# Tile 0's latent queries ahead of a half projection of tile 1 in layer 1, and five throw-away products left out

## The reference

```python
z = rms_norm(x) @ w_in            # 1184 columns: q, k, v of group A | latent queries cq (256) | ckv (128) | k_rope (32)
q_b = rms_norm(cq) @ b_w_uq       # 8 heads x 96, group B, multi-head latent attention
k_nope, v = split(ckv @ b_w_ukv)  # keys and values of group B out of the latent
o = concat(sliding_window_attention(q_a, k_a, v_a, sinks), latent_attention(q_b, k_nope, k_rope, v))
x = x + o @ w_o
x = x + swiglu(rms_norm(x))       # layer 0;  layer 1: top 2 of 8 SwiGLU experts, 2816 wide
```

## Time and profile before

| | |
|---|---|
| median of 3 runs | 1202.36 us (1201.98 to 1204.39) |
| profiled execution, own time | 1203.37 us |
| its span, first to last instruction | 1201.5 us |
| outside the span (difference) | 1.87 us |
| PE busy | 1179.6 us, 98% |
| DVE, ACT, POOL busy | 548.7, 329.9, 80.3 us |
| DMA | 348.56 MB, mean 290 GB/s |
| granted TensorE clock, mean | 0.999 |

### The profile page before, as it was taken

The page is one execution under the profiler, slowest core; times in us unless marked ns, Lnnn a source line. Parts: engine busy times, 40 slices in busy tenths (PEclk is TensorE's granted clock), DMA queues, the critical chain, the costliest instruction groups (busy, mean ns, idle before and its releaser), DMA issues.

```text
span 1201.5 us, 24345 instructions
## 1 busy us (share of the span) xinstructions
PE 1179.6 (98%) x10285; PEld 618.4 (51%) x10285; DVE 548.7 (46%) x1035; ACT 329.9 (27%) x612; POOL 80.3 (7%) x179
## 2 busy tenths in 40 slices
PE   8999999999999999999999999999999999999998
PEld 5566699999995566533333333333333333333254
DVE  2677534544414667533433434354264244334334
ACT  2576533443324556310210210210200200211101
POOL 4132000000001120000000000000000100100100
PEclk9999999999999999999999999999999999999999
DMA  9261294554530353999999999999999999999996
GB/s 304 60 168 37 92 285 150 174 175 132 162 125 1 63 132 125 352 369 375 406 389 413 398 399 413 399 398 414 399 396 415 399 399 415 390 408 414 392 410 256
DMA packets 114104, 348.56 MB, mean 290 GB/s; under 512 B 8592, under 2 KB 34032, under 8 KB 103808
## 3 DMA queue, kind: packets, MB, share of 16 engines
q1 hardware_dynamic: 108656, 335.55, 74.4%
q0 software_dynamic: 3648, 10.60, 3.1%
q10 hardware_dynamic: 1744, 1.61, 0.4%
HBM read 339.70 MB, written 8.04 MB: 289 GB/s over the span
## 4 chain that ended last, share of the span: by engine, by line
PE 86%; DMA 6%; DVE 4%; ACT 2%; SPq 1%; issue 1%; DVEq 0%; ACTq 0%
PE ps L2439 34%; PE ps L2446 17%; PE ps L2344 12%; PE ps L2075 8%; PE ps L2360 6%; DMA ring<-in_moe_w_gate 2%; DMA ring<-in_moe_w_down 2%; DMA ring<-in_w_in 2%; SPq L736 1%; PE ps L2274 1%; PE ps L2221 1%; PE ps L2236 1%; PE ps L2166 1%; PE ps L2155 1%; PE ps L2088 1%
## 5 line engine op out<-in xcount | busy, mean ns | idle before, releaser
L2439 PE MATMUL ps<-ring,xg 128*32 128x512 f32 (+1 forms) x1792 | 197.6, 547 | 1.2 <-DMA ring<-in_moe_w_gate 0.8
L1857 DVE STREAM_TRANSPOSE am<-act_m 32x256 f32<-32x256 f32 (+1 forms) x288 | 172.6, 599 | 4.7
L2439 PE MATMUL ps<-ring_more,xg 128*32 128x512 f32 (+1 forms) x1280 | 149.7, 571 | 0.0
L1351 DVE TENSOR_TENSOR w_lo<-ring,w_hi 128x2048 fp32r<-128x2048 f32 (+1 forms) x34 | 76.0, 2234 | 96.2 <-ACT w_hi L941 96.2
L2075 PE MATMUL ps<-ring,hT 128*128 128x512 f32 x256 | 115.4, 596 | 0.1
L2439 PEld LDWEIGHTS ps<-ring,xg 128*32 128x32 f32 x1792 | 58.0, 110 | 111.2 <-issue 106.4
L1842 DVE TENSOR_TENSOR act_m<-act_m,ps 64x512 f32<-64x512 f32 (+1 forms) x24 | 15.2, 635 | 213.1 <-ACT act_m L1290 213.1
L2439 PE MATMUL ps<-ring_more,am 128*32 128x512 f32 x896 | 108.9, 592 | 0.0
L2446 PE MATMUL ps<-ring,xg 128*32 128x512 f32 (+1 forms) x896 | 106.7, 547 | 0.0
L2344 PE MATMUL ps<-hT_hi,w_hi 128*128 128x288 f32 x352 | 104.3, 296 | 0.5 <-DVE hT_lo L1725 0.5
L2344 PE MATMUL ps<-hT_lo,w_hi 128*128 128x288 f32 x352 | 103.8, 295 | 0.0
(11 more groups left out here) (388 smaller groups left out, 1539.2 us busy)
## 6 DMA issues: line engine op xcount, KB each, us to landing
ring_more<-in_moe_w_down SPq DMA_DIRECT2D x64, 1024.0 KB, 16.0
ring<-in_moe_w_gate SPq DMA_DIRECT2D x48, 1024.0 KB, 17.0
ring_more<-in_moe_w_up SPq DMA_DIRECT2D x48, 1024.0 KB, 16.2
ring<-in_moe_w_gate SPq DMA_DIRECT2D x32, 768.0 KB, 18.6
ring_more<-in_moe_w_gate SPq DMA_DIRECT2D x16, 1024.0 KB, 14.7
ring<-in_moe_w_up SPq DMA_DIRECT2D x16, 1024.0 KB, 18.4
ring<-in_moe_w_down SPq DMA_DIRECT2D x16, 1024.0 KB, 15.5
ring<-in_moe_w_up SPq DMA_DIRECT2D x16, 768.0 KB, 14.7
```

The costliest lines, as they stand in the source:

```text
L1351: V.tensor_tensor(lo[:, 0:size], src[:, 0:size], hi[:, 0:size].bitcast(F32), ALU.subtract).then_inc(lo_ready, 1)
L1857: ins = V.transpose(am[GRAN * q:GRAN * q + GRAN, c % 2, 0:nk, GRAN * g:GRAN * g + GRAN], src)
L2439: ins = mm_(ps[GRAN * s_:GRAN * s_ + GRAN, b, 0:half], x[:, GRAN * g:GRAN * g + GRAN], w[:, half * h:half * h + half], start=(n == 0), sto ...
```

## The change

In layer 1 alone, three hand-written orders and one table are edited:

- PE: `(item, 4)` runs ahead of `(za, 1, 0, 1)`, and no longer behind it.
- ACT: `(isq, 4)` and `(ir, 4)` run ahead of `(zev, 1, 0)`, and `(ir, 4)` is no longer behind `(tie, 3)`.
- DVE: `(i2, 4)` runs ahead of `(sm, 1)`, and no longer behind it.
- `WAITING[1]` loses the entry for `(s, 2)`: five throw-away products, and the wait in front of them.

No step is added or dropped, and since `za` takes no small PSUM pair, every small step keeps its pair.

```diff
--- before.py
+++ after.py
@@ -113,8 +113,8 @@
              ("p", 7), ("o", 6), ("o", 7), ("hf", 0), ("wo", 1, 0, 0), ("wo", 1, 1, 1), ("wo", 1, 0, 1), ("hf", 1)],
             [("h", 0), ("tc",), ("item", 0), ("za", 0, 1, 0), ("h", 2), ("za", 2), ("titem", 0), ("za", 0, 0, 0), ("zc", 0),
              ("za", 0, 1, 1), ("za", 0, 0, 1), ("tq", 2), ("h", 1), ("item", 1), ("s", 0), ("za", 1, 0, 0), ("item", 2),
-             ("za", 1, 1, 0), ("tq", 0), ("za", 1, 1, 1), ("titem", 1), ("p", 0), ("item", 3), ("titem", 2), ("za", 1, 0, 1),
-             ("item", 4), ("titem", 3), ("s", 1), ("s", 2), ("titem", 4), ("o", 0), ("p", 1), ("s", 3), ("o", 1), ("zc", 1),
+             ("za", 1, 1, 0), ("tq", 0), ("za", 1, 1, 1), ("titem", 1), ("p", 0), ("item", 3), ("titem", 2), ("item", 4), ("za", 1, 0, 1),
+             ("titem", 3), ("s", 1), ("s", 2), ("titem", 4), ("o", 0), ("p", 1), ("s", 3), ("o", 1), ("zc", 1),
              ("ob", 1), ("p", 2), ("to", 2), ("o", 2), ("p", 3), ("wo", 2), ("o", 3), ("tq", 1), ("wo", 0, 0, 0), ("item", 5),
              ("item", 6), ("s", 4), ("wo", 0, 0, 1), ("titem", 5), ("s", 5), ("titem", 6), ("wo", 0, 1, 0), ("hf", 2), ("p", 4),
              ("s", 6), ("wo", 0, 1, 1), ("o", 4), ("p", 5), ("s", 7), ("ro", 2), ("o", 5), ("p", 6), ("wo", 1, 0, 0), ("o", 6),
@@ -131,8 +131,8 @@
               ("th", 2), ("th", 0), ("nh", 1), ("n2", 1), ("th", 1)],
              [("tce",), ("n1", 2), ("n1", 0), ("isq", 0), ("n1", 1), ("ir", 0), ("zev", 2), ("tie", 0), ("zr", 2), ("zcev", 0),
               ("zev", 0, 1), ("zev", 0, 0), ("tqe", 2), ("isq", 1), ("zr", 0), ("e", 0), ("ir", 1), ("isq", 2), ("tqe", 0),
-              ("ir", 2), ("zev", 1, 1), ("tie", 1), ("pe", 0), ("isq", 3), ("tie", 2), ("ir", 3), ("zev", 1, 0), ("isq", 4),
-              ("tie", 3), ("ir", 4), ("e", 1), ("tie", 4), ("pe", 1), ("e", 2), ("e", 3), ("zcev", 1), ("pe", 2), ("zr", 1),
+              ("ir", 2), ("zev", 1, 1), ("tie", 1), ("pe", 0), ("isq", 3), ("tie", 2), ("ir", 3), ("isq", 4), ("ir", 4), ("zev", 1, 0),
+              ("tie", 3), ("e", 1), ("tie", 4), ("pe", 1), ("e", 2), ("e", 3), ("zcev", 1), ("pe", 2), ("zr", 1),
               ("oe", 2), ("toe", 2), ("pe", 3), ("oe", 3), ("tqe", 1), ("n2", 2), ("isq", 5), ("ir", 5), ("isq", 6), ("ir", 6),
               ("tie", 5), ("e", 4), ("tie", 6), ("e", 5), ("pe", 4), ("e", 6), ("oe", 4), ("pe", 5), ("xd", 2),
               ("oe", 5), ("e", 7), ("pe", 6), ("oe", 6), ("pe", 7), ("n2", 0), ("oe", 7), ("xd", 0), ("xh", 2),
@@ -147,14 +147,14 @@
               ("hfd", 1), ("tl", 1)],
              [("hd", 0), ("x1", 2), ("hd", 2), ("i1", 0), ("i2", 0), ("r1", 0), ("r1", 1), ("set",), ("z1", 2), ("z2", 2),
               ("hd", 1), ("z1", 0), ("sm", 0), ("i1", 1), ("z2", 0), ("i2", 1), ("i1", 2), ("i2", 2), ("i1", 3), ("i2", 3),
-              ("i1", 4), ("sm", 1), ("i2", 4), ("sm", 2), ("od", 0), ("sm", 3), ("nm", 2), ("od", 1), ("z1", 1), ("nm", 3),
+              ("i1", 4), ("i2", 4), ("sm", 1), ("sm", 2), ("od", 0), ("sm", 3), ("nm", 2), ("od", 1), ("z1", 1), ("nm", 3),
               ("z2", 1), ("wd", 2), ("i1", 5), ("i2", 5), ("i1", 6), ("i2", 6), ("sm", 4), ("sm", 5), ("nm", 4), ("hfd", 2),
               ("nm", 5), ("sm", 6), ("wd", 0, 0), ("x2", 2), ("nm", 6), ("sm", 7), ("top", 2), ("wd", 0, 1), ("nm", 7),
               ("x2", 0), ("hfd", 0), ("wd", 1, 0), ("xl", 2), ("xl", 0), ("hfd", 1), ("top", 0), ("wd", 1, 1),
               ("hfdb", 1), ("rs", 1), ("x2h", 1), ("top", 1), ("x2", 1)]]
 
 WAITING = [{("h", 2): 4, ("h", 0): 2, ("h", 1): 1, ("p", 1): 1, ("o", 1): 4, ("s", 3): 1, ("p", 2): 3, ("o", 2): 2, ("hf", 1): 6},
-           {("s", 2): 5, ("o", 2): 1, ("p", 3): 2}]
+           {("o", 2): 1, ("p", 3): 2}]
 
 LATENT_FIRST = ((0, 1),)
 
```

## The result

The changed kernel takes 1206.4 us (median of 10 runs, 1204.62 to 1207.82), the kernel before 1203.08 (10 runs, 1201.98 to 1205.08): a ratio of 1.0024, interval 1.0016 to 1.0032, so 1.9 to 3.8 us slower. I had forecast 1202.4, in a range of 1200.2 to 1204.4, with most of the chance on no change. The profiled execution has an own time of 1205.34 and a span of 1203.5, against 1203.37 and 1201.5 before.

The account below looks back on a forecast made before the run. PE bounds attention, with expert transfers slightly behind PE setting the last 80 us. 2.6 us removed, 0.7 added at O0 and 1.8 to 2.0 in W2 sum to 0: forecast 1202.4 us, range 1200.2 to 1204.4.

Parts of the forecast that it names:

- Q0: Layer 1 attention, queries product of tile 0 on PE, (item, 4): 2.6 us long, to end near 409.6 ahead of ZA.
- ZA: Layer 1 attention, the moved half projection on PE, (za, 1, 0, 1): to end 2.6 us later, near 413.0.
- S2: Layer 1 attention, PE step (s, 2), behind the five removed products: to start near 414.5 without a wait, gaining 2.6 us.
- O0: Layer 1 attention, PE step (o, 0): to wait 0.7 us for ACT's exponentials, starting near 417.4.
- W2: Decode tile's output projection, (wo, 2): to start near 431.6, not 433.49, then wait 1.8 to 2.0 us for the last output weights.
- the sum of 0 for attention: Layer 1 attention: 2.6 us removed, 0.7 added at O0, 1.8 to 2.0 in W2; net -0.1 to +0.1, taken as 0.
- The first rival: Output weight loads are not in W2's way, so the gain of 1.9 us stays: 1200.5 us, chance 0.16.
- Removed 2.6: Sum's term for the five throw-away products ahead of S2 and the wait behind them: 2.6 us gained.
- from its end on all times are those of before: Sign of the forecast: from W2's end on, all times within 0.3 us of those before the change.
- a different length from 505 us on: Sign against the forecast, in the experts: a shift in attention would not pass one for one through them.
- The clock: Rival: idle PE at O0 and in W2 drops the granted clock to 1.2 GHz, costing 3.9 us: 1206.3, chance 0.05.
- S3: Layer 1 attention, scores of group 3 on PE, (s, 3), behind O0; the prediction gave it no term of its own.

Follow-up runs that it names:

- the padded kernel: Changed kernel with five throw-away products of 32 columns at PE's start, restoring the instruction count: 1204.13 us, ratio 1.0005.
- the kernel without products at its start: Kernel before with five throw-away products left out in layer 0, layer 1 untouched: 1206.03 us, ratio 1.0021.
- the last pair: Changed kernel with five thin products directly ahead of the expert loop, 1205.31 us, or behind the last expert, 1206.88 us.
- the version with W2 later: Changed kernel with W2 behind (tq, 1), tile 0's projection earlier, (n2, 2) later on ACT, two products at O0, three at PE's start: 1202.35 us, ratio 0.999.
- the one with one product of padding: Changed kernel with one throw-away product of 32 columns at PE's start, 16 instructions fewer than before: 1206.9 us, one execution.
- the one with four: Changed kernel with four throw-away products of 32 columns at PE's start, 4 instructions fewer than before: 1204.05 us, one execution.

## Why the prediction was wrong

**What held.** Q0 and ZA changed places at the times given, S2 started at 414.5 with no wait, O0 at 417.5 behind the exponentials (417.45 forecast). The loads of the output weights went out 2.6 us later and the last landed at 435.3 (435.4). The wait within W2 is there in the padded kernel, ended by the transfer of the output weights, 1.12 us long and not 1.8 to 2.0: W2's first 36 instructions took 2.35 us, not 2.06, and W2 started 0.2 us later than I had it (431.73, in an execution 0.08 us ahead). Its end, 437.1, is as forecast, because the landing sets it. So the sum of 0 for attention was right as far as full clock goes: the orders alone came out at 1.0000. The first rival, that the loads aren't in the way, fell: 22.7 us passed from their first issue to the last landing. The fit of the Trainium skill ("DMA: Bandwidth & Descriptors", "Anatomy of one DMA"), by which they would have been in long before, doesn't hold for them in the changed kernel either (11.6 us by the fit).

**The step that failed.** "Removed 2.6", the line on the five throw-away products. I costed them by the time that they take on PE and by the wait that they cover. They are also 20 instructions in PE's stream, and that I counted nowhere: the sum has no term for it, which put it at nothing without a reason. From there it went into "from its end on all times are those of before". With those 20 gone ahead of the loop over the experts, PE stops for about 3 us at the loop's exit. All fourteen kernels, both of the comparison among them, agree: the stop is there with 20, 16 and 8 instructions fewer ahead of the loop, wherever they were taken, and not with 4 or 0 fewer or 20 more. Its net price in the medians is 2.3 us by the padded kernel (1.0024 - 1.0005 of 1203), 2.5 by the kernel without products at its start, which has a thinner start too, and 2.4 by the last pair (1206.88 - 1205.31, and the 0.8 of the products ahead of the loop). The profiles put it at some 2 us where the clock holds behind the stop, because the transfers catch up, and at some 4 where it falls; the medians mix the two.

I did list "a different length from 505 us on" among what would prove me wrong, but read it as a shift that doesn't pass through. The shift passes, as the version with W2 later shows. What changed was the code's place. That attention as a whole came out at 0 was right by the mechanism and not by luck: the wait within W2 is there, if shorter than I had it.

**The rival that was partly true.** The clock. I gave it 0.05, with a fall behind W2's idle time, at 3.9 us. It falls earlier, behind O0's 0.87 us of idle time, where the granted clock was 0.58 for 4 us (a loss of 0.42 x 4 = 1.7 us, S3's 3.25 against 1.95 the most of it). In the profiled execution this cost next to nothing: W2 would have waited for its weights anyway. Seven profiled kernels have this wait at O0. Three of them show the fall: this one, the one with one product of padding (0.75 from 418 to 422, then 0.70 to 430) and the one with four (0.85, then 0.65). The other four stay at 1.00. What it costs in the median is bounded by the padded kernel's ratio of 1.0005 (0.6 us, interval -0.5 to 1.7), too near to zero to be called shown. My argument against this rival was a thin stretch at 426 to 430 with the clock at 1.00. It carries over badly to other places: 0.87 us of idle time at O0 went with 0.58, and 1.34 us ahead of S2 with 0.57.

**The account.** The measured median lies 4.0 us above the forecast of 1202.4. Of these, 0.7 are no effect of the change: I took the median of three runs of the kernel before, 1202.36, and ten give 1203.08. 3.3 us stand between the medians: 2.3 to 2.5 for the stop at the loop's exit with what the clock loses behind it, shown; the rest, 0.8 to 1, within what the clock's fall in attention can give, likely and not separated from scatter.

**Why the place decides, and what stays open.** Shown is that the stop stands at one place in the stream, and that with it one packet fewer is fetched up to 590 us and one more from 1100 us on. That holds in all fourteen kernels (33 and 8 fetches without the stop, 32 and 9 with it). One account fits both, and it is argued: a packet ends at that place. In the kernel before the place lies inside the loop, so the packet behind it is fetched in the loop's first pass, near 577 us, and is there when the loop ends. In the changed kernel the place lies behind the loop, so this packet is fetched only at the exit, and PE stands still until it is there. Both kernels have a fetch between 1106 and 1109 us, right at the exit, and only one stops; the row is the same in both:

```profile
q8 instruction: 1, 0.02, 2.3%
```

By this account the one kernel fetches ahead there and the other what it needs at once. Which instructions a packet carries isn't in the trace. Nor was it tried whether more than 20 fewer end the stop again.

## What to carry to other kernels

An edit that adds or takes instructions ahead of a loop moves the loop in the engine's stream, and that alone was worth 0.2% here. When a small edit gives a surprise of a few us, look in the profile for idle time ended by "issue" at a loop's exit, and put the same number of cheap instructions back at the start before blaming the edit. See, too, how many instructions run before the idle time: if that number moves with the padding, it is a place in the code that stops the engine, not a moment. Throw-away products can do three jobs (cover a wait, hold the clock, hold the code's place), and a gain ahead of a queued transfer stays a gain only if what waits for that transfer moves behind its landing.

## What the runs showed of the hardware

- Instructions come by DMA queues of their own, those taken here for PE's in packets of 0.02 MB, with none between 590 and 1100 us, while PE repeats a loop. Behind a loop of seven passes PE stood still for 2.77 to 3.60 us in the six kernels with 8 to 20 instructions fewer ahead of it, and not at all in the eight others. The stop stood at one place in the stream: behind 10, 6 and 0 instructions of the code that follows the loop, for 20, 16 and 8 fewer.
- The granted clock fell behind idle times as short as 0.87 us (three of seven profiles, 0.58 to 0.85 over the 4 us that follow) and 1.34 us (0.57), and stayed at 1.00 behind 2.58 us in another (products out). Behind the stop of some 3 us it fell in three of six. Two products of 256 columns at O0 went with no mean clock below 0.998 in 11 executions.
- A mean granted clock of 0.996 need not cost time: it can come from the kernel's start, where the same half pace is recorded as 0.50 in one execution and as 1.00 in another.
- In the last expert the loads are the bound: a stop of 3.05 us lengthened the span by 2.0, and the 1.27 us of waits for loads that were there before were gone.
